# Attention scores of a head's two halves as 64-row products in their own PSUM banks

## The chip, the cores and the metric

The kernel runs on one core of a Trainium2 chip. TensorE (PE in the profile) multiplies, with results in PSUM; ScalarE (ACT), VectorE (DVE) and GpSimd (POOL) do the rest, and SyncE's queue (SP) issues most DMAs. The metric is the device time of one execution in microseconds.

## What is computed

One layer of a hybrid model: a projection of 640 tokens (512 latent, 128 context) into the inputs of two mixers, retention and differential attention, then a gated merge, a router and 32 experts. The change touches the differential attention. Each of 8 heads has queries and keys in two halves of 64 dimensions; two softmaxes are formed and subtracted:

```python
DIFF_HEADS, DIFF_HD = 8, 64          # 512 latent tokens, 256 cached keys, 128 context tokens
s = jnp.einsum('bqhcd,bkhcd->bchqk', qblk, k).astype(F32) * scale   # c: the two halves
p = jax.nn.softmax(s, axis=-1)
a = p[:, 0] - lam * p[:, 1]
return jnp.einsum('bhqk,bkhe->bqhe', a, vf)
```

Latent queries see 768 keys (512 latent, 256 cached), context queries only the 128 context keys. Everything is fp32.

## The kernel before

The work is a list, `plan`, written out in order by the host program; each engine's program walks it and picks its own part, with semaphores between. Most of the list is dense products: `dense_item` for one tile of 128 tokens by 256 columns is 8 x 3 products (L838), since the operands are split in a high and a low part. Their results alternate between PSUM banks 0 and 1, and the product after the next waits until the bank was read (`wait_freed`). One section of 512 columns is two units of five such tiles (`mm`); `cv` is the rounding of the next unit's weights (ACT at L1252, then DVE at L1573).

The attention is put between dense products. There are 40 steps, (head h, token tile t), t = 0 to 3 latent and t = 4 (`PT`) context. `attention(0, ...)` runs 20 of them (heads 0 to 3) with 40 tiles of dense work, `attention(1, ...)` the other 20 with 20 tiles. For each step the list holds `S` (this step's scores), `AT` of the step before, this step's share of dense tiles, for t = 1 to 3 a part of the next head's preparation, and `PV` of the step before. On PE:

- preparation (`prep`, L871): four transposes each into bank 0 or 1, of the head's queries, keys, and the cached and context parts. ACT copies them out (L1166 to L1173). Keys go to `kT` (128 rows: 64 of the one half, 64 of the other). Queries go to `qz`, two tiles per head: one with the first 64 rows filled and the rest zero, one with the last 64 filled; `qzp` is the same for the context tile. DVE set the zeros once (L1631 to L1634).
- `S` (L985): queries as the loaded operand, keys as the moving one, for each half c two products, of 512 and 256 columns, into `score[c]`. The two scores lie one behind the other in banks 2, 3 and 4, so the third bank's first half is c = 0 and its second half c = 1. It waits until both exponentials of the step before are done (`exp_done`).
- DVE takes the maxima (L1641, L1642) and the bias (L1643); ACT takes the exponentials with their sums (L1279); DVE mixes them into `mixed` (L1647 to L1654).
- `AT` (L996): six transposes of `mixed` into banks 5 and 6, which ACT copies to `mixedT` (L1285, L1286), in its program behind this step's exponentials.
- `PV` (L1014; L1010 for a context tile): six products into bank 7, columns 0 to 127. ACT scales the result into `od` (L1150) and squares it into columns 128 to 255 of the same bank for a sum (L1296), and then counts `pv_read`.

The routing and the expert stage follow at the end. Experts' weights are loaded by SP's queue as PE's progress frees their places.

## Time and profile before

| | |
|---|---|
| timed runs, median of 3 | 1372.71 us (1371.94 to 1374.68) |
| the profiled execution | 1365.45 us |
| its span (first to last instruction) | 1363.5 us |
| PE busy | 1155.2 us, 85% of the span |
| PE's weight loads busy | 936.6 us |
| DVE busy | 500.0 us |
| ACT busy | 408.1 us |
| POOL busy | 101.3 us |
| all DMA | 222.28 MB, mean 163 GB/s |

Busy time of PE is the time in which at least one product was under way; products overlap, as each takes longer from start to end than the distance to the next. Weight loads have a line of their own (PEld) and overlap the products. The span has four parts: set-up and the first sections up to 411 us, the attention with its dense work up to 858 us (with sections of dense work alone from 607 to 698 us), the last projections and the routing up to 1061 us, and the experts.

### The profile page before, as it was taken

The numbers are of one execution on the slowest core, as the hardware profiler recorded it, in microseconds if no ns is written. First come the engines' busy times: TensorE is split into PE (matmuls) and PEld (weight loads), VectorE is DVE, ScalarE is ACT, GpSimd is POOL, SyncE is SP. The second block draws the span as 40 slices with busy tenths as digits, with TensorE's granted clock in tenths as the row PEclk, the third lists the DMA queues.
The fourth block names the chain that finished last, engine by engine and source line by source line (L and its number), as shares of the span: only waits on it lengthen the run. The fifth ranks groups of instructions, "written<-read, shape, count | busy, mean of one in ns | idle before, by whom it ended". The sixth has DMA issues, their size and how long they took to land. (4 is left out here: it accounts for less than half of the span.)

```text
span 1363.5 us, 19120 instructions
## 1 busy us (share of the span) xinstructions
PE 1155.2 (85%) x7969; PEld 936.6 (69%) x7969; DVE 500.0 (37%) x899; ACT 408.1 (30%) x878; POOL 101.3 (7%) x113
## 2 busy tenths in 40 slices
PE   2799999999979999999988998899972888787750
PEld 0488899889978998999977777798972533222210
DVE  0521116554433434433435445445556111111115
ACT  3522222122244454542244554413120121111113
POOL 0000000211000000000000000000000111111014
PEclk9799999999999999999999999899985799889985
DMA  8556632111311222232221101833219499999927
GB/s 308 215 184 204 200 94 62 62 39 49 115 48 58 65 69 79 63 111 68 76 87 47 47 22 34 356 139 105 78 62 385 164 402 421 421 420 421 420 95 222
DMA packets 90273, 222.28 MB, mean 163 GB/s; under 512 B 9881, under 2 KB 64962, under 8 KB 74706
## 3 DMA queue, kind: packets, MB, share of 16 engines
q1 hardware_dynamic: 84146, 205.41, 40.9%
q0 software_dynamic: 6048, 15.74, 3.6%
q8 instruction: 59, 0.97, 0.3%
q14 instruction: 20, 0.16, 0.0%
HBM read 206.41 MB, written 21.00 MB: 167 GB/s over the span
## 5 line engine op out<-in xcount | busy, mean ns | idle before, releaser
L838 PE MATMUL ps<-w_high,h_high 128*128 128x256 f32 x1280 | 369.7, 289 | 10.4 <-DVE arena L1499 5.2
L838 PE MATMUL ps<-w_high,h_low 128*128 128x256 f32 x1280 | 362.8, 283 | 0.0
L838 PE MATMUL ps<-w_low,h_high 128*128 128x256 f32 x1280 | 362.8, 283 | 0.0
L838 PEld LDWEIGHTS ps<-w_high,h_high 128*128 128x128 f32 x1280 | 246.1, 192 | 25.6 <-ACT arena L1224 10.1
L838 PEld LDWEIGHTS ps<-w_low,h_high 128*128 128x128 f32 x1280 | 246.3, 192 | 0.5 <-issue 0.2
L838 PEld LDWEIGHTS ps<-w_high,h_low 128*128 128x128 f32 x1280 | 246.1, 192 | 0.0
L1573 DVE TENSOR_TENSOR w_low<-w_loaded,w_high 128x2048 fp32r<-128x2048 f32 x44 | 100.8, 2291 | 171.8 <-ACT w_high L1252 171.8
L1042 PE MATMUL ps<-arena 128*64 128x512 f32 x512 | 124.8, 644 | 23.5 <-DMA arena<-in_moe_w_up 19.7
L1042 PEld LDWEIGHTS ps<-arena 128*64 128x64 f32 x512 | 40.2, 148 | 106.7 <-issue 106.7
L1224 ACT COPY arena<-ps 128x256 f32<-128x256 f32 x100 | 37.2, 372 | 247.6 <-PE ps L838 247.6
L1279 ACT ACTIVATE arena<-ps,neg_mx 128x768 f32<-128x768 f32 (+1 forms) x80 | 62.8, 790 | 134.2 <-DVE neg_mx L1643 134.2
L1252 ACT CAST w_high<-w_loaded 128x2048 fp32r<-128x2048 f32 x44 | 83.9, 1908 | 57.6 <-DMA w_loaded<-in_w_o 33.1
L985 PE MATMUL ps<-arena 128*128 128x256 f32 (+2 forms) x288 | 93.0, 464 | 3.2 <-ACT arena L1173 2.0
L1641 DVE TENSOR_REDUCE mx<-ps 128x1 f32<-128x768 f32 (+1 forms) x40 | 32.9, 823 | 96.9 <-PE ps L985 96.9
L1055 PE MATMUL ps<-arena 128*64 128x512 f32 x256 | 60.0, 611 | 9.8 <-ACT arena L1319 9.8
L985 PEld LDWEIGHTS ps<-arena 128*128 128x128 f32 x288 | 50.4, 191 | 22.4 <-issue 15.3
L1776 DVE SCALAR_TENSOR_TENSOR arena<-arena,ps 128x256 f32<-128x256 f32 x16 | 6.7, 421 | 143.6 <-ACT arena L1315 143.6
L1014 PE MATMUL ps<-arena 128*128 128x128 f32 x384 | 49.3, 278 | 11.8 <-ACT arena L1286 11.8
L1014 PEld LDWEIGHTS ps<-arena 128*128 128x128 f32 x384 | 45.5, 192 | 14.6 <-ACT arena L1286 14.6
L871 PE MATMUL ps<-const,arena 128*128 128x128 f32 x256 | 40.5, 286 | 13.6 <-POOL arena L1884 3.5
L838 PE MATMUL ps<-w_high,m_high 128*128 128x256 f32 x160 | 47.7, 298 | 2.7 <-DVE m_low L1541 0.8
L838 PE MATMUL ps<-w_high,od_high 128*128 128x256 f32 x160 | 46.3, 289 | 1.7 <-DVE od_whole L1470 0.9
(255 smaller groups left out, 1691.7 us busy)
## 6 DMA issues: line engine op xcount, KB each, us to landing
w_loaded<-in_w_in SPq DMA_DIRECT2D x32, 1024.0 KB, 5.6
arena<-in_moe_w_gate SPq DMA_DIRECT2D x32, 1024.0 KB, 14.3
arena<-in_moe_w_up SPq DMA_DIRECT2D x32, 1024.0 KB, 21.1
arena<-in_moe_w_down SPq DMA_DIRECT2D x32, 1024.0 KB, 20.2
arena<-in_w_ada SPq DMA_DIRECT2D x24, 1024.0 KB, 6.0
gates<-arena SPq DMA_DIRECT2D x40, 128.0 KB, 1.7
arena<-y_rows POOLq DMA_DIRECT2D x10, 512.0 KB, 8.1
arena<-in_x_sample SPq DMA_DIRECT2D x8, 512.0 KB, 10.8
```

The source lines that it names most:

```text
L838: mm = pe.matmul(out[:, 0:N256], x[:, t, k * P:(k + 1) * P], w[i % 2][:, k, :], start=(k == 0 and j == 0), stop=(k == KC - 1 and j == 2))
L871: mm = pe.transpose(out[:, k * P:(k + 1) * P], src[k], ident)
L985: mm = pe.matmul(score[c][:, lo:hi], q, keys, start=True, stop=True, skip_group_check=True)
L1014: mm = pe.matmul(B(7)[:, 0:P], mixedT[s % 2][:, k * P:(k + 1) * P], v, start=(k == 0), stop=(k == 5))
L1042: mm = pe.matmul(B(bank_at)[BLK * i:BLK * (i + 1), :].rearrange("p (g f) -> p g f", g=2), xgT[slot][:, k, BLK * i:BLK * (i + 1)], w_gu[e0 ...
L1055: mm = pe.matmul(B(5 + n)[BLK * i:BLK * (i + 1), :], act_aT[slot][:, k, BLK * i:BLK * (i + 1)], w_dn[e0 + i][:, k, n * N512:(n + 1) * N512 ...
L1224: free(act.copy(dst[:, t, c0:c0 + N256], src), n)
L1252: act.copy(w_hi[i % 2][:], w_raw[i % 2]).then_inc(w_rounded, 1)
L1279: act.activation(probs[:, c, 0:n], score[c][:, 0:n], ACT.Exp, bias=neg_mx[:, s % 2, c:c + 1], scale=DH ** -0.5, accum_out=den[:, s % 2, c: ...
L1573: dve.tensor_tensor(w_lo[i % 2][:], w_raw[i % 2], w_hi[i % 2][:].bitcast(F32), ALU.subtract).then_inc(w_split, 1)
L1641: dve.tensor_reduce(mx[:, 0:1], score[0][:, 0:n], AXX, ALU.max)
L1776: ins = dve.scalar_tensor_tensor(out=act_s[:, par, :], in0=act_t[:, par, :], scalar=1.0, in1=src[:, 0:FF], op0=ALU.add, op1=ALU.mult)
```

## The change

The queries are kept whole in one tile `qT` of 128 rows; `S` multiplies rows 0 to 63 of queries and keys for c = 0 and rows 64 to 127 for c = 1, in alternation. The zero-padded tiles and their memsets are gone, and ACT copies queries with one instruction where there were two. The two scores now have two banks each (2 and 3; 4 and 5). Therefore `AT` moves from banks 5 and 6 to banks 6 and 7, and the result of `PV` and its square move to columns 256 to 511 of bank 7, beside the last two transposes. Since they share that bank, `AT` now also waits for `pv_read` of the step before.

```diff
-        qz = [tiles(50 + 4 * i, 2, N512) for i in range(2)]
+        qT = [at(50 + 2.5 * i, N512 + P) for i in range(2)]
-        qzp = [at(65 + i, 2 * P).rearrange("p (c n) -> p c n", c=2) for i in range(2)]
...
-        score = [psf[:, 2 * N512:2 * N512 + KEYS], psf[:, 2 * N512 + KEYS:2 * N512 + 2 * KEYS]]
+        score = [psf[:, (2 + 2 * c) * N512:(2 + 2 * c) * N512 + KEYS] for c in range(2)]
+        pv_out, pv_square = B(7)[:, CTX:CTX + P], B(7)[:, CTX + P:CTX + 2 * P]
...
-                    for c in range(2):
-                        q = qz[h % 2][:, c, t * P:(t + 1) * P] if t < PT else qzp[h % 2][:, c, :]
-                        spans = [(0, 512), (512, 768)] if c == 0 else [(0, 256), (256, 768)]
-                        if t == PT:
-                            spans = [(0, P)]
-                        for lo, hi in spans:
-                            keys = kT[h % 2][:, lo:hi] if t < PT else kT[h % 2][:, KEYS:KEYS + P]
-                            mm = pe.matmul(score[c][:, lo:hi], q, keys, start=True, stop=True, skip_group_check=True)
+                        pe.wait_ge(o_read, NT)
+                    spans = [(0, 0, N512), (1, 0, N512), (0, N512, KEYS), (1, N512, KEYS)] if t < PT else [(0, 0, P), (1, 0, P)]
+                    for c, lo, hi in spans:
+                        r = slice(c * DH, (c + 1) * DH)
+                        keys = kT[h % 2][r, lo:hi] if t < PT else kT[h % 2][r, KEYS:KEYS + P]
+                        mm = pe.matmul(score[c][:, lo:hi], qT[h % 2][r, t * P:(t + 1) * P], keys,
+                                       start=True, stop=True, skip_group_check=True)
...
                     if s:
                         pe.wait_ge(at_read, s)
+                        pe.wait_ge(pv_read, s)
                     else:
                         pe.wait_ge(o_read, NT)
+                        pe.wait_ge(u_read, 2 * len(UPDATES))
                     for k in range(6 if t < PT else 1):
-                        mm = pe.transpose(B(5 + k // 4)[:, (k % 4) * P:(k % 4 + 1) * P], mixed[:, k * P:(k + 1) * P], ident)
+                        mm = pe.transpose(B(6 + k // 4)[:, (k % 4) * P:(k % 4 + 1) * P], mixed[:, k * P:(k + 1) * P], ident)
...
-                            act.copy(qz[h % 2][0:DH, 0, :], src[0:DH, :])
-                            ins = act.copy(qz[h % 2][DH:P, 1, :], src[DH:P, :])
+                            ins = act.copy(qT[h % 2][:, 0:N512], src)
...
-                            act.copy(qzp[h % 2][0:DH, 0, :], src[0:DH, 3 * P:4 * P])
-                            ins = act.copy(qzp[h % 2][DH:P, 1, :], src[DH:P, 3 * P:4 * P])
+                            ins = act.copy(qT[h % 2][:, N512:N512 + P], src[:, 3 * P:4 * P])
...
-                    scale_copy(od[:, t, h * P:(h + 1) * P], B(7)[:, 0:P], rden[:, s % 2, 0:1])
-                    act.activation(B(7)[:, P:2 * P], B(7)[:, 0:P], ACT.Square, scale=rden[:, s % 2, 0:1],
+                    scale_copy(od[:, t, h * P:(h + 1) * P], pv_out, rden[:, s % 2, 0:1])
+                    act.activation(pv_square, pv_out, ACT.Square, scale=rden[:, s % 2, 0:1],
...
-                    for i in range(2):
-                        dve.memset(qz[i][DH:P, 0, :], 0.0)
-                        dve.memset(qz[i][0:DH, 1, :], 0.0)
-                        dve.memset(qzp[i][DH:P, 0, :], 0.0)
-                        ins = dve.memset(qzp[i][0:DH, 1, :], 0.0)
-                    setp(ins)
+                    n_set[0] += 1
+                    dve.sem_inc(dve_set, 1)
```

On PE, at the fourth and fifth attention step (S of head 0, t = 3 and t = 4, with PV and AT around them), before the change. L985 are scores, L996 transposes of `mixed`, L1014 the PV products; the program's numbers in front of the rows show that 50 rows (dense products and the preparation's transposes) stand between AT and PV:

```order
2534 L985 MATMUL ps<-arena 128x512 [waits exp_done]
2535 L985 MATMUL ps<-arena 128x256 x2
2536 L985 MATMUL ps<-arena 128x512
2537 L996 MATMUL ps<-const,arena 128x128 [waits at_read,mixed_ready]
2538 L996 MATMUL ps<-const,arena 128x128 x5
...
2589 L1014 MATMUL ps<-arena 128x128 [waits pv_read,at_read]
2590 L1014 MATMUL ps<-arena 128x128 x5
2591 L985 MATMUL ps<-arena 128x128 [waits exp_done]
2592 L985 MATMUL ps<-arena 128x128
2593 L996 MATMUL ps<-const,arena 128x128 [waits at_read,mixed_ready]
```

The same place after the change, where the lines are L983, L997 and L1013:

```order
2534 L983 MATMUL ps<-arena 128x512 [waits exp_done]
2535 L983 MATMUL ps<-arena 128x512
2536 L983 MATMUL ps<-arena 128x256 x2
2537 L997 MATMUL ps<-const,arena 128x128 [waits pv_read,at_read,mixed_ready]
2538 L997 MATMUL ps<-const,arena 128x128 x5
...
2589 L1013 MATMUL ps<-arena 128x128 [waits pv_read,at_read]
2590 L1013 MATMUL ps<-arena 128x128 x5
2591 L983 MATMUL ps<-arena 128x128 [waits exp_done]
2592 L983 MATMUL ps<-arena 128x128
2593 L997 MATMUL ps<-const,arena 128x128 [waits pv_read,at_read,mixed_ready]
```

The wide score products now come first and the narrow ones last, and the wait for `pv_read`, which PV had, stands one place earlier as well, at the first transpose.

On ACT, the copies of a head's preparation at the first step, before and after (L1166 to L1173, now L1165 to L1170):

```order
142 L1167 COPY arena<-ps 64x512
143 L1169 COPY arena<-ps 128x512 [waits pe_dense]
144 L1171 COPY arena<-ps 128x384 [waits pe_dense]
145 L1172 COPY arena<-ps 64x128
146 L1173 COPY arena<-ps 64x128
147 L1279 ACTIVATE arena,den<-ps,neg_mx 128x768 [waits max_ready]
```

```order
141 L1165 COPY arena<-ps 128x512 [waits dve_set,pe_dense]
142 L1167 COPY arena<-ps 128x512 [waits pe_dense]
143 L1169 COPY arena<-ps 128x384 [waits pe_dense]
144 L1170 COPY arena<-ps 128x128
145 L1276 ACTIVATE arena,den<-ps,neg_mx 128x768 [waits max_ready]
```

Two copies fewer stand in front of the exponentials; nothing else moved there.

## Rows read from the trace of the kernel before

**Rows 1.** Windows: us of stretch; busy us (instructions) by engine, granted clock, DMA share, GB/s

```profile
411.10:606.50 195.40, 195.38 (x1438) 177.44 (x1438) 77.91 (x128) 92.64 (x236) 7.90 (x9) 1.00 0.22 65
698.40:858.00 159.60, 142.12 (x959) 120.63 (x960) 80.59 (x152) 77.25 (x203) 7.89 (x9) 1.00 0.13 42
...
1100.00:1200.00 100.00, 84.88 (x396) 31.49 (x392) 11.73 (x20) 16.32 (x34) 13.35 (x14) 0.97 1.01 415
```

**Rows 2.** Groups by form, scores: records | busy us, mean ns | idle before

```profile
L985 PE MATMUL ps<-arena 128*128 128x512 f32 x128 | 65.7, 595 | 3.2 <-ACT arena L1173 2.0 <-ACT arena L1279 1.2
L985 PE MATMUL ps<-arena 128*128 128x256 f32 x128 | 32.8, 379 | 0.0
```

**Rows 3.** Waits of PE, 700 to 870 us: total us, times, longest

```profile
PE ps L1014 <- ACT arena L1286: 11.8, 12, 1.6
```

**Rows 4.** Timeline, one long step, second half: start us, us, engine, operation [idle before]

```profile
763.59 2.75 PE L985 MATMUL ps<-arena 128*128 128x512 f32 x8
...
763.93 2.29 DVE L1573 TENSOR_TENSOR w_low<-w_loaded,w_high 128x2048 fp32r<-128x2048 f32 x1 [0.74 <-ACT w_high L1252]
...
764.76 0.24 ACT L1296 ACTIVATION_READ_ACCUMULATOR ps<-ps,rden 128x1 f32 x1
766.17 0.82 PE L996 MATMUL ps<-const,arena 128*128 128x128 f32 x6
766.38 0.96 DVE L1641 TENSOR_REDUCE mx<-ps 128x1 f32<-128x768 f32 x1 [0.15 <-PE ps L985]
...
770.67 0.39 ACT L1286 COPY arena<-ps 128x256 f32<-128x256 f32 x1
...
771.11 1.60 PE L1014 MATMUL ps<-arena 128*128 128x128 f32 x12 [0.80 <-ACT arena L1286]
...
772.55 0.61 PE L985 MATMUL ps<-arena 128*128 128x128 f32 x4
```

**Rows 5.** Timeline of PE around one group of 32-column products (L805)

```profile
107.47 0.28 PE L838 MATMUL ps<-w_high,h_low 128*128 128x256 f32 x1
107.68 1.06 PE L805 MATMUL ps<-arena 128*32 128x512 f32 x8
108.67 0.38 PE L838 MATMUL ps<-w_high,h_high 128*128 128x256 f32 x1
108.90 0.28 PE L838 MATMUL ps<-w_low,h_high 128*128 128x256 f32 x1
109.02 0.28 PE L838 MATMUL ps<-w_high,h_low 128*128 128x256 f32 x1
```

**Rows 6.** Timeline of weight loads in the expert stage, two 64-column products alternating

```profile
1153.10 0.15 PEld L1042 LDWEIGHTS ps<-arena 128*64 128x64 f32 x2 [0.28 <-issue]
1153.53 0.15 PEld L1042 LDWEIGHTS ps<-arena 128*64 128x64 f32 x2 [0.28 <-issue]
```

**Rows 7.** Timeline of DVE, second half: a split and the maximum; a maximum alone

```profile
707.02 1.29 DVE L1541 TENSOR_TENSOR o_low<-o_whole,o_high 128x512 fp32r<-128x512 f32 x2
708.22 0.95 DVE L1641 TENSOR_REDUCE mx<-ps 128x1 f32<-128x768 f32 x1
...
757.41 0.96 DVE L1641 TENSOR_REDUCE mx<-ps 128x1 f32<-128x768 f32 x1 [3.19 <-PE ps L985]
```

**Rows 8.** Timeline of a short step (t = 4), first half

```profile
451.85 0.61 PE L985 MATMUL ps<-arena 128*128 128x128 f32 x4
452.29 0.82 PE L996 MATMUL ps<-const,arena 128*128 128x128 f32 x6
...
452.98 0.26 ACT L1173 COPY arena<-ps 64x128 f32<-64x128 f32 x1
...
453.78 0.20 ACT L1296 ACTIVATION_READ_ACCUMULATOR ps<-ps,rden 128x1 f32 x1
```

**Rows 9.** Timeline of a short step, second half, whose scores start at 772.55

```profile
773.27 0.20 ACT L1296 ACTIVATION_READ_ACCUMULATOR ps<-ps,rden 128x1 f32 x1
```

**Rows 10.** Timeline of PE at the start of the second half

```profile
696.79 0.66 PE L871 MATMUL ps<-const,arena 128*128 128x128 f32 x4 [1.45 <-ACT arena L1167]
...
698.44 2.85 PE L985 MATMUL ps<-arena 128*128 128x512 f32 x8 [1.00 <-ACT arena L1173]
```

More of the change, by code:

```diff
@@ L1004, in _ @@
                         pe.wait_ge(pv_read, s)
-                    else:
-                        pe.wait_ge(u_read, 2 * len(UPDATES))
                     if t == 0:
@@ L1009, in _ @@
                     if t == PT:
-                        mm = pe.matmul(B(7)[:, 0:P], mixedT[s % 2][:, 0:P], dv[:, PT, c0:c0 + P], start=True, stop=True)
+                        mm = pe.matmul(pv_out, mixedT[s % 2][:, 0:P], dv[:, PT, c0:c0 + P], start=True, stop=True)
                     else:
@@ L1013, in _ @@
                             v = dv[:, k, c0:c0 + P] if k < 4 else ctx_v[:, k - 4, c0:c0 + P]
-                            mm = pe.matmul(B(7)[:, 0:P], mixedT[s % 2][:, k * P:(k + 1) * P], v, start=(k == 0), stop=(k == 5))
+                            mm = pe.matmul(pv_out, mixedT[s % 2][:, k * P:(k + 1) * P], v, start=(k == 0), stop=(k == 5))
                     mm.then_inc(pe_pv, 1)
@@ L1284, in _ @@
                     if steps[s][1] < PT:
-                        act.copy(mixedT[s % 2][:, 0:N512], B(5))
-                        act.copy(mixedT[s % 2][:, N512:KEYS], B(6)[:, 0:CTX]).then_inc(at_read, 1)
+                        act.copy(mixedT[s % 2][:, 0:N512], B(6))
+                        act.copy(mixedT[s % 2][:, N512:KEYS], B(7)[:, 0:CTX]).then_inc(at_read, 1)
                     else:
-                        act.copy(mixedT[s % 2][:, 0:P], B(5)[:, 0:P]).then_inc(at_read, 1)
+                        act.copy(mixedT[s % 2][:, 0:P], B(6)[:, 0:P]).then_inc(at_read, 1)
                 elif e[0] == "PV":
```

## Prediction

> **What bounds the kernel now.** I read first the busy time of each engine by stretch [rows 1]. The scores belong to the attention of two halves of four heads each, 411 to 606 us and 698 to 858 us. In the first half TensorE (PE) is busy all the time (195.38 of 195.40 us), so a microsecond taken off PE there is a microsecond off the kernel. In the second it is busy 142.12 of 159.60 us, so something else sets the pace at times. The granted clock is 1.00 in both, the 2.4 GHz level. The stretch from 1100 us, in the expert stage, has the DMA share at 1.01: weights bound it. But those loads are issued as PE frees buffers, after a routing that needs the attention. So an earlier end of the attention shifts the whole tail; it is not swallowed by it.
>
> Second, the forms of the score products [rows 2]. 32 of the 40 steps have 768 keys, four instructions each; fp32 makes two passes of each, hence 128 records of 512 columns and 128 of 256. Eight steps (the context tokens, t = 4) have only 128 keys. The records of the long steps fill 65.7 + 32.8 = 98.5 us of PE.
>
> Third, what PE waits for in the second half [rows 3]: 12 times for the copies of `mixedT` (L1286), 11.8 us in all. The chain in order of time [rows 4] says why. Scores start at 763.59; VectorE (DVE) takes maxima from 766.38; ScalarE (ACT) does both exponentials and, behind them, the copies that end at 770.67 + 0.39; only then PV starts (771.11), and 772.55 is the next step's start. That loop of 8.96 us holds the scores once, in series. In the second half they lie on this loop, in the first half on PE's own queue: in both they set the time.
>
> **The long score products.** From the first score pass to the first transpose behind it are 766.17 - 763.59 = 2.58 us [rows 4]: eight passes one after another, 0.43 us for 512 columns and 0.215 us for 256. The trace has no 64-row products. The nearest rows are those that use a part of the array's columns [rows 5, 6]. L805 issues four products of 32 columns in places of their own; with their second passes they are eight records, and the next product starts 108.67 - 107.68 = 0.99 us later. In series they would need 3.44. So four products run at once, and all first passes come ahead of the second ones. L1042 alternates two of 64 columns, and a pair of weight loads appears every 0.43 us, inside the products: two streams, loads hidden. I take the same for two halves of rows, as they use other rows and other banks: 2 x 0.43 + 2 x 0.215 = 1.29 us.
>
> Going into such a group and out of it costs something, by the same rows [rows 5]: the start comes 0.21 us after the last whole product instead of 0.12 (+0.09), the exit 0.99 - 0.86 = 0.13, and the second product behind it 0.23 instead of 0.12 (+0.11). Sum 0.33 us per group. In front of transposes the last part may be less. New length 1.29 + 0.33 = 1.62, so a long step gives back 0.96 to 1.0 us of PE time; I take 1.0. The Trainium skill, TensorEngine Tiling (Array Packing), Key Properties, says that changing the tiling mode drains the TensorE, a rule against this change, as all neighbours of the scores use the whole array; the trace agrees, with this 0.33 us. Without it the sum would be 32 x 0.33 = 10.6 us larger.
>
> First half, PE's queue: 16 x 1.0 = **16.0 us**.
>
> Second half, the loop: there the time from start to the last pass's end counts. Before: last pass from 2.15 us, 512 wide, mean 0.595 [rows 2]. After: entry 0.09, last pass from 1.08, 256 wide, 0.379. Gain 2.745 - 1.549 = 1.20 us. PE has 0.8 us of idle per such loop and gains 1.0 itself, so it stays behind the chain. But DVE must be free for the maxima. At 763.93 it starts a weight split of 2.29 us, to 766.22 [rows 4], so this step gains only 766.38 - 766.22 = 0.16; three steps are like that. In two earlier steps DVE already goes straight from the splits into the maximum (707.02 + 1.29, then 708.22) and gains nothing. In the other eleven it had idled for the scores (3.19 us at 757.41) [rows 7]. So 11 x 1.20 + 3 x 0.16 = **13.7 us**.
>
> **The new wait.** The transposes of `mixed` now fill banks 6 and 7, and PV's result moved beside them, so AT waits for `pv_read`: ACT must have scaled and squared the PV of the step before. Behind AT on PE stand the dense products, PV and the next scores. In a long step AT now comes 1.5 us after the old start of the scores. `pv_read` comes at 764.76 + 0.24 = 1.41 us in a step where ACT does a weight cast first [rows 4], mostly at 0.92: covered, with 0.1 to 0.6 us to spare. In the eight short steps there is no cover. First half [rows 8]: scores at 451.85, read done at 453.98, 2.13 us later; one of ACT's two small copies ahead of it (0.26) goes, so 1.87, and AT starts at some 1.92 instead of 452.29 - 451.85 = 0.44. That costs 1.48 x 4 = 5.9 us in a stretch where PE is never idle. Second half [rows 9]: read done at 773.27 + 0.20, 0.92 after 772.55, so AT at 0.97 instead of 0.45, 0.52 x 4 = 2.1 us; PV of these steps waits for nothing else, so it counts. Entry and exit of the short groups fall under this wait. Together **-8.0 us**.
>
> **The rest.** ACT copies q whole instead of in two halves: per head one copy of 0.58 us and one of 0.26 us less. The other heads' copies lie beside other work. At the second half's start they are the queue that PE waits for, 1.45 and 1.00 us [rows 10]: +0.84; at the first, +0.26. **+1.1 us.** The eight memsets of zero padding ran on DVE long before the first scores, beside dense products; I give them 0. The wait for `o_read` in the first score step is on work long done: 0. Maxima and exponentials read the same 768 columns per half, from whole banks: 0.
>
> **Sum.** 16.0 + 13.7 - 8.0 + 1.1 = 22.8 us. The profiled execution took 1365.45 us (span 1363.5 and 1.95 around it), which becomes 1342.65. The three timed runs have a median of 1372.71, 7.26 us more; the gain moves with it unchanged: **1349.9 us**.
>
> **Bounds.** If two loads of 128 columns can't be taken together, each costs PE some 0.12 us (PV's 12 passes of 128 columns: 771.11 to 772.55), 0.24 per pair against rounds of 0.215: about 0.2 us per step with the first pair, 27 steps, 5.4 us: 1355. If exit costs nothing beyond 0.13, +1.8: 1348. If ACT's copies shift so that the long steps keep 1.3 us and the short ones wait 0.5 less: 1344. Own range 1344 to 1356.
>
> **Rivals.**
> *Passes in program order.* If the second pass of the first half had to go before the first pass of the other, a step would take 0.43 x 3 + 0.43 for the 256-wide rest = 1.72 instead of 1.29: 27 x 0.43 = 11.6 us less gain, 1361.5. Against it: by that order L805's group would take 5 x 0.43 = 2.15, not 0.99 [rows 5].
> *ACT late in the long steps.* The margin of AT is 0.1 us where ACT has a cast. If ACT, whose work per step is the same in a shorter step, falls 0.3 us behind in all of the 27: 8.1 us less, 1358.
> *No overlap by rows, the slower side.* Nothing in the trace shows two halves of rows at once. If they run one after another, the passes stay at 2.58 us and the change of mode is paid: first half 16 x 0.33 = 5.3 us more, second half (0.09 entry, but a last pass shorter by 0.21) 11 x 0.12 = 1.3 less, the new wait 8.0 more, the copies 1.1 less: 1372.7 + 10.9 = 1383.6. It decides as soon as the overlap saves less than 0.3 us per step.
> *Clock.* More waiting on PE could bring the 1.2 GHz level into the attention. The second half holds 1.00 with 11% of PE idle [rows 1]; each 2 us at the lower level cost 1, and 45 us of it would eat all: about 1372.
> *Full doubling.* If switching cost nothing and the waits were covered, 32 x 1.29 = 41.3 us: 1331.4. The Trainium skill, TensorEngine Tiling (Array Packing), Theoretical Speedup, gives up to 2x for a contraction of 64 or less, which is this case.
>
> **Chances.** Forecast 0.70, program order 0.05, ACT late 0.08, full doubling 0.04, clock 0.05, no overlap 0.08. The range 1342 to 1362 holds the first three, 0.83. A measurement tells 0.2% (2.7 us) from no change; faster by more: 0.70 + 0.05 + 0.08 + 0.04 = 0.87; within: 0.05; slower: 0.08.
>
> **What would show it.** In the profile after, the scores' records of 512 and 256 columns should fill some 45 to 50 us of PE instead of 98.5, and their first transposes start 1.4 to 1.5 us behind them. PE should show waits for the line of the square (now L1293) in the short steps, near 1.4 us in the first half and 0.5 in the second, and none in the long ones. The loop of 8.96 us should be 7.7 to 7.8, and 8.8 where the weight split comes. The long steps of the first half should be 1.0 us shorter. I am wrong if the scores still take over 2 us, if long steps wait for `pv_read`, or if the expert stage, unchanged in length, starts less than 20 us earlier.

## The result, and the profile after

| | before | after |
|---|---|---|
| timed runs, median of 4 | 1373.03 us (1371.94 to 1374.68) | 1350.20 us (1347.13 to 1351.80) |
| ratio, 95% interval | | 0.983 [0.981, 0.985] |
| the profiled execution | 1365.45 us | 1347.13 us |
| its span | 1363.5 us | 1345.3 us |
| PE busy | 1155.2 us | 1128.6 us |

The change takes 22.8 us off the median, 1.7%. The forecast was 1349.9 us, with a range of 1342 to 1362. The two profiled executions differ by less, 18.2 us of span; where the rest comes from is the subject of the last experiment.

Windows of the profile after, over the same work as in [rows 1] (columns as there):

```profile
410.95:597.75 186.80, 180.74 (x1437) 164.77 (x1437) 78.33 (x128) 91.06 (x232) 7.92 (x9) 1.00 0.23 69
688.30:838.90 150.60, 128.92 (x957) 109.03 (x957) 80.57 (x152) 75.02 (x198) 7.89 (x9) 0.99 0.14 46
1083.00:1183.00 100.00, 84.30 (x396) 31.36 (x392) 11.74 (x20) 16.33 (x34) 13.18 (x14) 0.97 1.01 414
```

The first half of the attention took 195 us and takes 187; the second took 160 and takes 151. In the first half PE was never idle and now is, for 6 us. The expert stage is what it was, and comes 18 us earlier. From the first transpose behind the attention (L871, the one that POOL's result releases, at 862.34 us before and 844.35 after) to the end it is 501.2 us before and 501.0 after: the gain is not swallowed by the weights' DMAs, and not enlarged.

The score products by form, with the transposes, the products behind them and their idle time, all after (records | busy us, mean ns | idle before, releaser):

```profile
L983 PE MATMUL ps<-arena 64*128 64x512 f32 x128 | 36.1, 641 | 2.5 <-ACT arena L1170 1.5 <-ACT arena L1276 1.0
L983 PE MATMUL ps<-arena 64*128 64x256 f32 x128 | 19.1, 376 | 0.0
L997 PE MATMUL ps<-const,arena 128*128 128x128 f32 x200 | 30.9, 286 | 9.5 <-ACT ps L1293 9.5
L1013 PE MATMUL ps<-arena 128*128 128x128 f32 x384 | 49.8, 280 | 13.3 <-ACT arena L1283 13.3
```

The records of the long steps fill 55.2 us of PE instead of 98.5 [rows 2], with as many of them and nearly the same time for one. So 43 us of score time are gone from PE, but only some 19 of them from the kernel. One part of what was given back stands in the third line: a new wait of 9.5 us in front of the transposes (L997) for ACT's square (L1293). The wait in front of PV in the fourth line hardly grew, 13.3 us where there were 11.8 [rows 3]. The larger part shows in no wait: entering and leaving 32 groups of 64-row products, some 11 us at the 0.34 us of one that is measured below, and about 4 us in five steps in which DVE is busy when the scores are ready.

**A long step of the first half, after.** Timeline (start us, us, engine, operation [idle before]):

```profile
438.07 0.30 PEld L983 LDWEIGHTS ps<-arena 64*128 64x128 f32 x4
438.07 1.56 PE L983 MATMUL ps<-arena 64*128 64x512 f32 x8
...
438.60 0.19 PEld L983 LDWEIGHTS ps<-arena 64*128 64x128 f32 x2 [0.24 <-issue]
...
439.03 0.19 PEld L983 LDWEIGHTS ps<-arena 64*128 64x128 f32 x2 [0.23 <-issue]
439.56 0.64 PEld L997 LDWEIGHTS ps<-const,arena 128*128 128x128 f32 x6 [0.33 <-issue]
439.56 0.88 PE L997 MATMUL ps<-const,arena 128*128 128x128 f32 x6
439.68 0.96 DVE L1634 TENSOR_REDUCE mx<-ps 128x1 f32<-128x768 f32 x1 [4.39 <-PE ps L983]
```

Eight passes in 439.56 - 438.07 = 1.49 us, where [rows 4] had 2.58. A round is two passes side by side, one on each half of the rows. The weight loads come in pairs, one pair per round: those at 438.60 and 439.03 are 0.43 us apart. But the first round took 438.60 - 438.07 = 0.53 us, and the last one, of 256 columns, is followed by the transposes 0.09 us later than its own 0.21. The step's distance to the next is 9.83 us instead of 10.77.

**The loop of the second half, after**, in a step without a weight split (columns as above):

```profile
741.19 1.56 PE L983 MATMUL ps<-arena 64*128 64x512 f32 x8
...
742.79 0.96 DVE L1634 TENSOR_REDUCE mx<-ps 128x1 f32<-128x768 f32 x1 [2.11 <-PE ps L983]
...
747.53 1.60 PE L1013 MATMUL ps<-arena 128*128 128x128 f32 x12 [0.67 <-ACT arena L1283]
...
749.07 1.13 PE L983 MATMUL ps<-arena 64*128 64x512 f32 x4
```

and the next one, where DVE has a weight split (L1570):

```profile
749.31 2.29 DVE L1570 TENSOR_TENSOR w_low<-w_loaded,w_high 128x2048 fp32r<-128x2048 f32 x1 [0.74 <-ACT w_high L1249]
...
751.52 0.95 DVE L1634 TENSOR_REDUCE mx<-ps 128x1 f32<-128x768 f32 x1
...
757.78 0.49 PE L983 MATMUL ps<-arena 64*128 64x128 f32 x4
```

A count below 8 in the last line of a view (x4 here, x2 further on) only means that the view ends inside the group. The loop of 8.96 us is 7.88 (749.07 - 741.19); with the split it is 8.71 (757.78 - 749.07). The scores are ready at 749.07 + 1.6, and DVE reads them at 751.52: the maximum no longer waits for PE there but for DVE's own queue.

**A short step of the first half, after:**

```profile
447.89 0.49 PE L983 MATMUL ps<-arena 64*128 64x128 f32 x4
...
449.33 0.23 ACT L1293 ACTIVATION_READ_ACCUMULATOR ps<-ps,rden 128x1 f32 x1
...
449.70 0.84 PE L997 MATMUL ps<-const,arena 128*128 128x128 f32 x6 [1.32 <-ACT ps L1293]
```

The transposes start 1.81 us behind the scores, against 0.44 in [rows 8], with 1.32 us of plain idle time released by the square. This is the new wait for `pv_read`.

**The end of a half, after**, which the forecast had not looked at:

```profile
597.43 0.20 ACT L1293 ACTIVATION_READ_ACCUMULATOR ps<-ps,rden 128x1 f32 x1
...
597.78 0.30 PE L997 MATMUL ps<-const,arena 128*128 128x128 f32 x1 [0.90 <-ACT ps L1293]
```

The last transpose of a half has the PV of the step before directly in front of it, with no scores and no dense tile between. It always waits for the whole reading of that PV.

### The profile page after: what moved, and what is told of

It is laid out like the page before. It is cut to its first block and busy times, and to the rows that moved or that the text cites. A ratio compares the mean times of both kernels' runs of the same rounds, so it can differ in the third digit from the quotient of the medians.

```text
span 1345.3 us, 19096 instructions
## 1 busy us (share of the span) xinstructions
PE 1128.6 (84%) x7969; PEld 914.0 (68%) x7969; DVE 497.7 (37%) x891; ACT 402.1 (30%) x862; POOL 101.3 (8%) x113
## 5 line engine op out<-in xcount | busy, mean ns | idle before, releaser
L838 PE MATMUL ps<-w_high,h_high 128*128 128x256 f32 x1280 | 369.4, 289 | 10.5 <-DVE arena L1496 5.2
L838 PE MATMUL ps<-w_low,h_high 128*128 128x256 f32 x1280 | 362.9, 283 | 0.0
L838 PE MATMUL ps<-w_high,h_low 128*128 128x256 f32 x1280 | 362.8, 283 | 0.0
L838 PEld LDWEIGHTS ps<-w_high,h_high 128*128 128x128 f32 x1280 | 246.3, 192 | 24.9 <-ACT arena L1221 10.1
L838 PEld LDWEIGHTS ps<-w_low,h_high 128*128 128x128 f32 x1280 | 246.3, 192 | 0.2
L838 PEld LDWEIGHTS ps<-w_high,h_low 128*128 128x128 f32 x1280 | 246.1, 192 | 0.0
L1570 DVE TENSOR_TENSOR w_low<-w_loaded,w_high 128x2048 fp32r<-128x2048 f32 x44 | 100.8, 2291 | 174.5 <-ACT w_high L1249 174.4
L1041 PE MATMUL ps<-arena 128*64 128x512 f32 x512 | 126.2, 650 | 22.8 <-DMA arena<-in_moe_w_up 19.1
L1013 PE MATMUL ps<-arena 128*128 128x128 f32 x384 | 49.8, 280 | 13.3 <-ACT arena L1283 13.3
L1013 PEld LDWEIGHTS ps<-arena 128*128 128x128 f32 x384 | 45.9, 193 | 16.1 <-ACT arena L1283 16.1
L983 PE MATMUL ps<-arena 64*128 64x256 f32 (+2 forms) x288 | 54.2, 490 | 2.5 <-ACT arena L1170 1.5
L871 PE MATMUL ps<-const,arena 128*128 128x128 f32 x256 | 40.4, 286 | 13.1 <-POOL arena L1877 3.5
L838 PE MATMUL ps<-w_high,m_high 128*128 128x256 f32 x160 | 48.2, 301 | 2.5 <-DVE m_low L1538 0.8
L838 PE MATMUL ps<-w_high,o_high 128*128 128x256 f32 x160 | 47.0, 293 | 0.8 <-DVE o_low L1538 0.8
L1312 ACT ACTIVATE arena<-ps 128x256 f32<-128x256 f32 x16 | 6.1, 384 | 137.7 <-PE ps L1041 137.7
## 6 DMA issues: line engine op xcount, KB each, us to landing
arena<-in_moe_w_gate SPq DMA_DIRECT2D x32, 1024.0 KB, 12.8
arena<-in_x_sample SPq DMA_DIRECT2D x8, 512.0 KB, 10.9
```

Of the source, the lines that this page charges most:

```text
L838: mm = pe.matmul(out[:, 0:N256], x[:, t, k * P:(k + 1) * P], w[i % 2][:, k, :], start=(k == 0 and j == 0), stop=(k == KC - 1 and j == 2))
L871: mm = pe.transpose(out[:, k * P:(k + 1) * P], src[k], ident)
L983: mm = pe.matmul(score[c][:, lo:hi], qT[h % 2][r, t * P:(t + 1) * P], keys, start=True, stop=True, skip_group_check=True)
L1013: mm = pe.matmul(pv_out, mixedT[s % 2][:, k * P:(k + 1) * P], v, start=(k == 0), stop=(k == 5))
L1041: mm = pe.matmul(B(bank_at)[BLK * i:BLK * (i + 1), :].rearrange("p (g f) -> p g f", g=2), xgT[slot][:, k, BLK * i:BLK * (i + 1)], w_gu[e0 ...
L1570: dve.tensor_tensor(w_lo[i % 2][:], w_raw[i % 2], w_hi[i % 2][:].bitcast(F32), ALU.subtract).then_inc(w_split, 1)
```

## Experiments

### The banks alone

Padded products of 128 rows as before, but with the new banks, the new order of the products and the wait for `pv_read`:

```diff
-                        r = slice(c * DH, (c + 1) * DH)
-                        keys = kT[h % 2][r, lo:hi] if t < PT else kT[h % 2][r, KEYS:KEYS + P]
-                        mm = pe.matmul(score[c][:, lo:hi], qT[h % 2][r, t * P:(t + 1) * P], keys,
+                        q = qz[h % 2][:, c, t * P:(t + 1) * P] if t < PT else qzp[h % 2][:, c, :]
+                        keys = kT[h % 2][:, lo:hi] if t < PT else kT[h % 2][:, KEYS:KEYS + P]
+                        mm = pe.matmul(score[c][:, lo:hi], q, keys,
```

> The changed kernel with the zero-padded 128-row products of before (and their copies and memsets), so only the banks and the wait of the transposes for pv_read are changed against before. Theory (the new wait stands in the open in the short steps): first half 4 x 1.7 us, second half 4 x 0.5, the last transposes of each half 0.6 each, less 11 x 0.2 where the last score pass is now narrow and the chain sets the pace: 7.8 us slower than before, 1381, and waits for the line of the square in ten places. Rival (another product or ACT takes the delay up): 1373, no change against before.

Measured: 1382.09 us (1381.11 to 1384.00), ratio 1.0072 [1.0051, 1.0093]: 9.6 us slower. Its wait at the transposes:

```profile
PE ps L998 <- ACT ps L1296: 10.0, 10, 1.7
```

(us in total, times, longest). These are the ten places that the theory named. So the new arrangement by itself costs what the forecast said and a little more. The gain comes from the row halves and, for some 2 us, from the copies that fall away with the padding (0.8 us at the start of the second half, the rest in the short steps). The long steps of the first half are 10.77 us as before and the loop of the second 8.96. The short steps lose 1.86 us each in the first half; ACT still has the two copies more in front of its reading here, which makes it 0.37 more than in the changed kernel. By the distances between like instructions, without the 1.7 us that each of two low-clock stretches costs there, the arrangement costs 10.9 us. The expectation of 7.8 had the ends of the halves in it, 0.6 us each, and they are that; what it missed is the gain of 11 x 0.2 us, which did not come, and 0.9 us more in the short steps.

It also corrects a term. The forecast took the end of the pass of 256 columns as nearer than that of 512, and priced the slower rival with 0.21 us of gain for it. But the narrow pass starts 0.215 us later: the loop stayed at 8.96. The order of the products is worth nothing.

### Both halves on the same rows

The 64-row form, the same records and the same changes of mode, but both halves on rows 0 to 63, so that nothing can run beside the other. The scores of the second half of each head are left out (the first is computed twice).

```diff
-                        r = slice(c * DH, (c + 1) * DH)
+                        r = slice(0, DH)
```

> The changed kernel, but both score products of a head use rows 0 to 63, so that they can't run side by side; the second half's scores are left out (those of the first half stand twice). Theory (all of the gain is the overlap of the two groups of rows): long scores take 2.6 us from first pass to transposes, plus the change of mode, and the kernel is slower than before by 10 to 12 us, 1384. Rival (64-row products are cheaper than 128-row ones by themselves, or the gain is in the banks and copies): at or below 1373.

Measured: 1388.37 us (1381.98 to 1394.61), ratio 1.012 [1.0074, 1.0166]. A long step of it (timeline, PE):

```profile
425.03 2.85 PE L983 MATMUL ps<-arena 64*128 64x512 f32 x8
...
427.80 0.88 PE L997 MATMUL ps<-const,arena 128*128 128x128 f32 x6
```

The passes are in series again, 2.77 us to the transposes instead of 2.58, and a long step takes 11.107 us against 10.770 before. The passes behind the first follow each other at the old distances (0.43 and 0.215 us). So the difference, 0.34 us, is the price of a group of 64-row products among whole ones, with the overlap taken away. The trace agrees with the rule that the forecast weighed (the Trainium skill, TensorEngine Tiling (Array Packing), Key Properties: a change of tiling mode drains the TensorE), and 0.34 us is its size here.

### One half after the other in the program

```diff
-                    spans = [(0, 0, N512), (1, 0, N512), (0, N512, KEYS), (1, N512, KEYS)] if t < PT else [(0, 0, P), (1, 0, P)]
+                    spans = [(0, 0, N512), (0, N512, KEYS), (1, 0, N512), (1, N512, KEYS)] if t < PT else [(0, 0, P), (1, 0, P)]
```

> The changed kernel with the four products of a long step in the order: first half 512, first half 256, second half 512, second half 256 columns, in place of alternation. Theory (each group of rows has its own queue of passes, so that only what is ready matters): no change against the changed kernel, 1350, passes of both groups start within 0.1 us. Rival (a pass can overtake only its own instruction's second pass; a following instruction on the same rows holds up the rest): the second half's products start after 0.9 us or more, a long step is 0.6 to 1.1 us longer, 27 of them on the path: 1366 to 1380.

Measured: 1349.19 us (1348.48 to 1349.91), ratio 0.9836 [0.9816, 0.9856], the same as the changed kernel.

```profile
431.50 1.57 PE L983 MATMUL ps<-arena 64*128 64x512 f32 x8
...
433.00 0.87 PE L997 MATMUL ps<-const,arena 128*128 128x128 f32 x6
```

1.50 us again. The first product of the second half of rows starts 0.013 us behind that of the first half, although the program has two products of the first half in front of it, with two passes each. So the alternation is not what makes them overlap; the two halves of rows proceed each by itself over at least this distance. This removes the rival of passes in program order more strictly than [rows 5] could.

### The wait for PV one bank later

Only the fifth and sixth transpose share a bank with PV's result, so the wait can stand in front of the fifth:

```diff
                         pe.wait_ge(at_read, s)
-                        pe.wait_ge(pv_read, s)
...
                     for k in range(6 if t < PT else 1):
+                        if s and k == 4:
+                            pe.wait_ge(pv_read, s)
```

> The changed kernel with the wait for pv_read moved from the first transpose to the fifth, the first one that writes bank 7; the one transpose of a context step never waits. Theory (the wait is on the path in all eight short steps and behind both last steps): eight times 0.44 us of transposes now lie ahead of the wait and the two ends lose 0.6 us each: 4.7 us faster than the changed kernel, 1345.5. Rival (the wait is hidden by the chain in the second half): half of it, 1348.

Measured: 1345.78 us (1345.09 to 1348.65), ratio 0.9817 [0.9794, 0.9839]; 4.4 us below the changed kernel, for 4.7 expected; from the first scores to the transpose behind POOL the traces differ by 5.1 us (432.3 and 427.1).

```profile
PE ps L998 <- ACT ps L1294: 2.7, 5, 0.6
```

The wait falls from 9.5 us to 2.7, the short steps' loss from 1.49 to 0.99 us in the first half and from 0.64 to 0.14 in the second, and the ends of the halves wait no longer. The wait is a real part of the time, not a pause that something else would have filled.

### The weight split one tile later

```diff
-                if t == 2 and i + 1 < len(UNITS):
+                if t == (3 if s[:2] == "wr" else 2) and i + 1 < len(UNITS):
```

> The changed kernel (1350.2 us), with one order altered in the second half of the attention: the rounding of the next unit's weights (ACT's cast, then DVE's split of 2.29 us) comes one tile later, so that the split falls beside the scores of a short step and not of a long one. The profile of the changed kernel has four long steps in which DVE is in the split when the scores are ready; they take 8.72 us where the eleven others take 7.88. If DVE alone holds these four, as the forecast had it, they fall to 7.9: 4 x 0.84 = 3.4 us less; the short steps have narrow maxima and some room, and give back 0 to 0.5 each. Expected 1347.5, between 1346.8 and 1349. Rival: what holds these steps is ACT (its cast of the weights sits in front of its reads of PV) or the loop as such; then they stay at 8.7 and the time at 1350.

Measured: 1349.08 us (1348.15 to 1357.32), ratio 0.9838 [0.9806, 0.9869]; not told apart from the changed kernel. Yet the steps named did what the theory said: all four long steps with a split fell to 7.88 us, three of them from 8.72 and the first from 9.75 (the expectation had put all four at 8.72). DVE held them. The gain came back in the short steps. One of them, first in the changed kernel and then with the later split, each under its own fence:

```profile
757.78 0.49 PE L983 MATMUL ps<-arena 64*128 64x128 f32 x4
...
758.75 0.85 PE L997 MATMUL ps<-const,arena 128*128 128x128 f32 x6 [0.48 <-ACT ps L1293]
```

```profile
759.66 1.93 ACT L1249 CAST w_high<-w_loaded 128x2048 fp32r<-128x2048 f32 x1
...
761.37 0.49 PE L983 MATMUL ps<-arena 64*128 64x128 f32 x4
...
761.62 2.29 DVE L1570 TENSOR_TENSOR w_low<-w_loaded,w_high 128x2048 fp32r<-128x2048 f32 x1 [0.74 <-ACT w_high L1249]
...
762.89 0.85 PE L997 MATMUL ps<-const,arena 128*128 128x128 f32 x6 [1.03 <-ACT ps L1293]
...
763.82 0.28 DVE L1634 TENSOR_REDUCE mx<-ps 128x1 f32<-128x128 f32 x1
...
766.45 1.50 PE L1013 MATMUL ps<-arena 128*128 128x128 f32 x12
...
767.88 0.70 PE L983 MATMUL ps<-arena 64*128 64x512 f32 x2
```

This short step takes 6.51 us where it took 5.96. The split does hold its maximum until 763.82, but that costs nothing here: PV starts at 766.45 without idle time in front of it. What costs is the cast that comes with the split. It stands on ACT until 761.59, in front of a preparation's copies and of the reading of PV, and so the transposes wait 1.03 us for the square where they waited 0.48. These 0.55 us are the whole lengthening of the step. So the rival that the expectation named for the long steps, ACT's cast in front of its reads of PV, is what lengthens the short ones, and the room for the maxima that I had expected is there. Only in the last short step, whose reading is not late, does the held maximum count, with 0.24 us. The first one loses most, 9.04 us for 5.96: its transposes start 1.59 us later, and a stretch of 3.4 us at the lower clock (from 725.9) falls into it.

### Two groups per step

The late wait, and the two products of 256 keys behind the fourth transpose instead of behind the products of 512, in 30 long steps. The same products, but twice the changes of mode. Where the step before is a short one, with one transpose, they come behind that one. In `AT`, where `later` holds the two narrow products of the step whose wide ones were just issued:

```diff
                         mm = pe.transpose(B(6 + k // 4)[:, (k % 4) * P:(k % 4 + 1) * P], mixed[:, k * P:(k + 1) * P], ident)
+                        if later and k == (3 if t < PT else 0):
...
+                            score_products(later).then_inc(pe_scores, 1)
+                            later = []
```

> The kernel of the late wait (1345.8 us), with each long step's scores cut in two groups: the two products of 512 keys where they were, the two of 256 keys behind the fourth transpose of mixed. Nothing is computed that was not, but in 30 long steps TensorE goes from whole-array to 64-row products and back twice instead of once. This doubles the disputed price of a group by itself. Theory: a group costs 0.33 to 0.4 us (a later start, a first round of 0.53 instead of 0.43, a slower exit). Then the long steps of the first half, bound by TensorE, go from 9.83 to 10.2 us: 15 x 0.36 = 5.4 more. In the second half the maxima also start four transposes later, 0.43 + 0.24 in 11 steps = 7.4 more, so 1358.6 in all. Rival: changing costs nothing, and the 0.06 us per long step that the forecast missed are DVE's or ACT's; then the first half is unchanged and the second loses 11 x 0.43 = 4.7: 1350.5.

Measured: 1357.57 us (1356.79 to 1359.30), ratio 0.9884 [0.9864, 0.9904]. Timeline of PE in one step:

```profile
440.75 1.13 PE L984 MATMUL ps<-arena 64*128 64x512 f32 x4
441.81 0.66 PE L1003 MATMUL ps<-const,arena 128*128 128x128 f32 x4
...
442.39 0.70 PE L984 MATMUL ps<-arena 64*128 64x256 f32 x4
...
443.03 0.44 PE L1003 MATMUL ps<-const,arena 128*128 128x128 f32 x2
```

Passes worth 0.86 us take 1.06, and passes worth 0.43 take 0.64: each group has the same 0.20 us on top, whatever its width, besides its later start. From the first scores to the last transpose the first half took 183.74 us with one group per step and takes 189.17 with two: 5.43 / 15 = 0.36 us for a group. The theory expected 5.4. In the second half the loss was 6.6 us, for 7.4 expected.

### The transposes of a short step behind a dense tile

The late wait, and in the short steps of the first half `AT` comes behind the first dense tile of the step:

```diff
-                if j:
+                behind = 1 if j and t == PT and half == 0 else 0
+                if j and not behind:
                     plan.append(("AT", s - 1))
-                for item in share[j]:
+                for n, item in enumerate(share[j]):
                     emit(item)
+                    if behind and n == 0:
+                        plan.append(("AT", s - 1))
```

> The kernel of the late wait (1345.8 us), and in the short steps of the first half the transposes of mixed come behind the step's first dense tile instead of right behind the scores. There the wait for pv_read still cost about 0.98 us in each of four steps; the dense tile (5 us) covers it, and the copies behind the transposes have another tile in front of PV. Expected -3.8 us: 1342, between 1341 and 1343.5. Rival: the copies and PV come too late then, and PE waits for them at PV instead: 1345.8 or more.

Measured: 1341.45 us (1341.18 to 1342.52), ratio 0.9762 [0.9743, 0.9781]. Its short step:

```profile
448.90 0.49 PE L986 MATMUL ps<-arena 64*128 64x128 f32 x4
...
452.29 0.82 PE L1001 MATMUL ps<-const,arena 128*128 128x128 f32 x6
...
457.25 0.70 PE L986 MATMUL ps<-arena 64*128 64x512 f32 x2
```

The median is 4.3 us below that of the late wait alone, for 3.8 expected. The two were timed in different sets of runs, beside which before took 1372.49 and 1374.76; from the first scores of the first half to those of the second the traces give 3.2 us (275.1 and 271.9). The step takes 8.35 us (late wait alone 9.18, changed kernel 9.68, before 8.19). The dense tile covers ACT's reading, and PV further on still finds its copies done: no idle time stands in front of the transposes or of PV here.

### All three

> The late wait, the late transposes in the short steps of the first half, and the later weight split of the second half together. Each is meant to take away one of the places at which the gain of the 64-row scores was given back or not collected. If they are independent: 1345.8 - 3.8 - 3.0 = 1339 us, between 1337.5 and 1341. If the split beside a short step delays that step, whose wait for pv_read has nothing in front of it, 1342.

Measured: 1340.41 us (1337.74 to 1343.45), ratio 0.9757 [0.9736, 0.9777]. This is the fastest median, but not told apart from the 1341.45 without the moved split. The time lies between the two cases of the expectation, but the steps show which holds. Three long ones gain 0.84 us and the first 1.87; of the short steps with a split the first loses 1.90 and the next two 0.85 each (6.32 against 5.46). From its first scores to its last transpose the second half takes 146.43 us here and 146.42 with the late wait alone: the later split is worth nothing. The late wait and the late transposes are the version to keep: 33.3 us below the 1374.76 that before took beside them, where the change alone gave 22.8.

### The same kernels once more

Before and after, unchanged, to see where 22.8 and 18.2 us part.

> The kernel before, unchanged, profiled again. The two profiled executions differ by 18.2 us of span, the medians by 22.8. The profiled executions of seven of the eight other kernels of this study hold a stretch of about 6.8 us at the 1.2 GHz level near 290 us, before the attention, and the two with long score products (the banks alone, the same rows) another at 414 to 416 us. Theory: the profiled execution of before (1365.45) was one without either, and a usual one has both, up to 3.4 us each: 1372.3. Expected here: granted clock under 1.00 near 290 and near 415 us, about 1372. Rival: the clock is as in the first profile and the time 1365 to 1366, or the 7 us lie at another place (the DMAs of the expert stage).

> As the other new profile of before: if the place of the low clock belongs to the kernel and not to chance, the same two stretches near 290 and 415 us and about 1372 us. If it is chance, another pattern.

> The changed kernel, unchanged, profiled again. Theory: the stretch at the lower level near 290 us is there (3.4 us more than the 1347.13 of its first profile), none near 415 us, since none of the kernels with short score products showed one: about 1350. Rival: it has both or neither, and the pairs of executions differ by chance alone: 1347 or 1354.

Measured: before 1372.95 and 1374.65 us, after 1352.63. Windows of 255 to 305 us (columns as in [rows 1]; the granted clock is the third number from the end), first of before in its first profile, then of the two new ones, each under its own fence:

```profile
255.00:305.00 50.00, 45.18 (x313) 42.47 (x312) 27.61 (x62) 10.08 (x20) 9.25 (x8) 1.00 0.16 48
```

```profile
255.00:305.00 50.00, 45.18 (x298) 42.70 (x297) 27.52 (x61) 8.88 (x17) 9.25 (x8) 0.93 0.16 48
```

```profile
255.00:305.00 50.00, 45.83 (x292) 43.41 (x291) 28.33 (x62) 8.89 (x17) 9.24 (x8) 0.90 0.16 48
405.00:425.00 20.00, 15.56 (x98) 12.71 (x97) 7.15 (x14) 7.74 (x21) 0.00 (x0) 0.91 0.18 53
```

And of the changed kernel profiled again:

```profile
255.00:305.00 50.00, 45.80 (x292) 43.38 (x291) 27.97 (x62) 8.89 (x17) 9.24 (x8) 0.90 0.16 48
```

The theory holds in its first half. The first profiles of both kernels had 1.00 in this stretch, the new ones have less. The first scores start at 411.1 us there and at 414.2 and 416.2 us in the new ones of before, and at 411.0 and 415.6 us in those of the changed kernel: 3 to 5 us lost before the attention begins, in either kernel. Up to 1.5 us of it is there before 290 us: the 501st dense product (L838) starts at 133.3 us in the first profile of before and at 134.7 in the last. Its second half falls: near 415 us only one of the two new profiles of before is low; the other is low for 3.4 us at 701.6 instead. By chance or not, each of the two loses 1.7 us within the attention.

What is the change worth, then? From the first scores to the transpose that POOL's result releases it is 451.2 us in the first profile of before, and 432.3 in the second profile of after; both ran at 1.00 but for their last two microseconds. So the program itself gained 19.0 us (18.95 unrounded). The other 3.8 us of the medians' difference are in no step of the program. The new profiles of before took 452.9 and 453.0 us for the same stretch, and 503.9 and 503.5 us behind it where the first took 501.2; the changed kernel took 501.0 and 502.9 behind it. So differences of this size come and go with the low-clock stretches. But no profile of a median execution exists, and that the clock accounts for the 3.8 us is not shown. Whether the changed kernel gets fewer such stretches for a reason, or had luck in four runs, stays open.

## The prediction, point by point

**The mechanism** was right: two halves of rows run side by side, the gain is PE's queue in the first half and the loop in the second, and one new wait gives a third of it back. All five marks that it named for the profile came, two of them a little outside their numbers: 55.2 us for the scores' records, over the 45 to 50 that it said (the two forms overlap and are counted apart; by the timeline a group is 1.56 us, 50 for 32), transposes 1.49 us behind them (1.4 to 1.5), waits for the square in the short steps and none in the long ones with one exception (2.50 us behind the scores at 711.33, where ACT has casts and a preparation's copy in front of the reading; the trace of before already had that reading at 2.44, and I had not looked at it), the first half's long steps shorter by 0.94 (1.0), and the loop at 7.88 (7.7 to 7.8), 8.72 with the split (8.8). Of its three signs of being wrong two were touched: one long step does wait for `pv_read`, and the tail of the kernel, unchanged in length, starts 18.0 us earlier in the first pair of profiles, under the 20 of that sign. The first cost nothing (the step takes 9.75 us with the late wait too). The second goes with the sum of 19.0 us below, where the forecast had 22.8.

**The sizes**, from the distances between the first score passes of two steps, before against the two profiles of after:

| term | forecast | measured |
|---|---|---|
| long steps, first half | +16.0 | +15.1 (16 x 0.94) |
| long steps, second half | +13.7 | +12.4 |
| short steps' wait | -8.0 | -8.2 |
| last transposes of the halves | 0 | -1.2 |
| ACT's copies | +1.1 | +0.8 |
| sum, without what the clock did | 22.8 | 19.0 |

The rounded terms of the last column add up to 18.9, the unrounded ones to 19.0.

- The group's price of 0.33 us, taken from the products of 32 columns [rows 5], is 0.34 and 0.36 in the two experiments that isolate it. I had then rounded the gain of 0.96 up to 1.0, because "the last part may be less" in front of transposes. It was not less: 0.9 us too much.
- The loop gained 1.08 us instead of 1.20 (seven of the eleven steps; three gained 0.99, the first 1.28). The step of the argument that was off is "last pass from 1.08": in the first round after the change of mode the second passes come 0.53 us behind the first ones and not 0.43, so the last pass starts 1.19 us in. The three steps with a split gained 0.24 instead of 0.16, and the two that DVE already bound gained 0 and -0.1, as forecast.
- The wait was sized well in sum (8.2 for 8.0): 1.49 us three times and 1.25 in the first half (1.48 four times in the forecast), 0.64 three times and 0.52 in the second (0.52 four times). In the second half the transposes come where the forecast had them, 0.97 us behind the scores. The 0.12 above that are the entry of the next group: PV's first product stands 1.43 us ahead of the next scores instead of 1.34. I had let entry and exit of the short groups vanish under the wait; the exit does, the entry stands on the other side of it.
- The last transposes were missed: they start 1.06 us later each for `pv_read`, of which 0.47 come back since ACT's copy behind them no longer has that reading in front of it: 2 x 0.59 = 1.2 us. A wait has to be followed to every place where the instruction stands, not only to those inside the loop.

**The time** was hit within 0.3 us by more luck than these terms deserve. Their sum should have been 19.0, 1353.7 us by the same way of shifting the median; the difference is in no term of the forecast. The lower clock, which it carried along unchanged, is the likely place, but that is not shown.

**The rivals.** Program order: excluded by one half after the other. No overlap: with both halves on the same rows it was 1388, where the forecast said 1383.6; it had the right sign, but a loop shorter by 0.12 us, where the loop got longer by 0.19. ACT late: not in the long steps, but for the one exception, which cost nothing. Clock: both levels are seen, yet the stretches do not grow with PE's idle time; the changed kernel, with more of it, has 0.99 and 1.00 in the second half. Full doubling: the passes themselves go from 2.58 to 1.29 us by their distances, so the factor of up to 2 (the Trainium skill, TensorEngine Tiling (Array Packing), Theoretical Speedup) holds for them; with the group's price it is 2.58 to 1.64.

## What to carry to other kernels

A contraction of 64 is worth splitting by rows where the group is long: its saving here is 1.29 us, and it pays 0.35 us for each time that whole-array products become half-array ones and back, however long the group is. The short groups of 128 columns lose by it: with the late wait a short step of the second half takes 5.46 us where before took 5.32, with no wait in it. Price a new bank arrangement as an edit of its own: here it cost 9.6 us alone, and moving one wait by four instructions and one set of transposes behind a tile of dense work brought back 8.8 by the medians, 8.3 by the traces. And before moving a block out of one step's way, look at what moves with it: here the cast on ACT went with the split on DVE, and came to stand in front of a reading that TensorE waits for.

## What the hardware showed that I had not expected

- **Products on the two halves of rows start 0.01 us apart and proceed independently**, even where the program has the two products of one half ahead of the other (1.50 us in both orders). fp32 with its two passes takes part in it.
- **The first weight load of a group of 64-row products is not hidden.** Before, among whole-array products, the first load starts 0.11 us ahead of the first score pass. This is the same place of the loop as in [rows 4]:

```profile
763.48 0.30 PEld L985 LDWEIGHTS ps<-arena 128*128 128x128 f32 x2
763.59 2.75 PE L985 MATMUL ps<-arena 128*128 128x512 f32 x8
```

After, both start together at 438.07. The first passes are recorded with 0.69 us instead of the 0.59 of the next ones, and the second passes come 0.53 us behind them and not 0.43. The loads for the second passes are not what delays these: they end 0.30 us into the first. With it the price of a group is told in full: 0.09 us of later start, 0.10 of this round, 0.10 between the last pass and the first transpose, and 0.06 between that and the second, 0.34 to 0.35 together. That the passes wait for their load is read from the times alone; no run took it away.
- **The same kernel on the same work has its low-clock stretches at different places**: of before, near 290 and 702 us in one execution, 270, 294 and 416 in another, and none between 55 and 861 us in the first. Each takes 3.4 to 6.8 us at 1.2 GHz and costs up to half of that. The six pairs that can be made of the three profiles of before and the two of after differ by 12.8 to 27.5 us, while the program gained 19.0. The distances between like instructions at the same clock repeat within 0.02 us.
